# Four array quadrants per batch of 64x64 products in a chunked RWKV-7 step, and one projection step moved between the transposes

## The reference, cut

```python
SEQ = 512; HEAD_SIZE = 64; N_HEADS = 16; DEC_BATCH = 8; D_FF = 2816
def rwkv7_recurrence(state0, r, w, k, v, kk, a):
    def step(S, inp):
        r_t, w_t, k_t, v_t, kk_t, a_t = inp
        sa = jnp.einsum('bhvk,bhk->bhv', S, kk_t)
        S = (S * w_t[:, :, None, :]
             - sa[..., None] * (kk_t * a_t)[:, :, None, :]
             + v_t[..., None] * k_t[:, :, None, :])
        y = jnp.einsum('bhvk,bhk->bhv', S, r_t)
        return S, y
def token_mixer(h, shift_prev, wkv_prev, pool_prev, pos0, l, p):
    proj = jnp.einsum('btd,de->bte', h, w_in)          # r | k | v | loras | pool | gates
    y, S_new = rwkv7_recurrence(wkv_prev, r_h, hs(decay), k_h, v_h, kk_h, hs(a))
    y = ((y - mu) * lax.rsqrt(var + GN_EPS)).reshape(B, T, D_RWKV) * p['gn_w'][l] + p['gn_b'][l]
    ...
```

## Time and profile before

| | us |
|---|---|
| median of 3 runs (1501.89 to 1502.12) | 1501.95 |
| the profiled execution | 1501.0 |
| its span, first to last instruction | 1499.2 |
| PE busy | 1257.2 |
| DVE busy | 718.3 |
| ACT busy | 483.7 |

### The profile page before, as it was taken

The page is one execution under the profiler, slowest core; times in us unless marked ns, Lnnn a source line. Parts: engine busy times, 40 slices in busy tenths (PEclk is TensorE's granted clock), DMA queues, the critical chain, the costliest instruction groups (busy, mean ns, idle before and its releaser), DMA issues. The chain is left out here.

```text
span 1499.2 us, 34641 instructions
## 1 busy us (share of the span) xinstructions
PE 1257.2 (84%) x15148; PEld 1140.8 (76%) x15148; DVE 718.3 (48%) x1101; ACT 483.7 (32%) x771; POOL 87.1 (6%) x145
## 2 busy tenths in 40 slices
PE   4777999999999998678599999526999999699953
PEld 1377888888888887565599999516999999699952
DVE  2334455555555544377233232284666666722226
ACT  0343333432434323322322222104544444322211
POOL 0002021120210202010000000000000000000000
PEclk9889999999999999785699999857999999899985
DMA  8131011010110100359623232312222222133221
GB/s 276 64 85 47 4 47 49 2 49 10 41 49 2 35 2 4 116 126 291 203 86 90 84 91 74 125 56 57 85 84 84 84 84 84 38 105 89 77 85 64
DMA packets 185345, 117.26 MB, mean 78 GB/s; under 512 B 6624, under 2 KB 177430, under 8 KB 184935
## 3 DMA queue, kind: packets, MB, share of 16 engines
q1 hardware_dynamic: 185233, 115.58, 26.3%
HBM read 108.40 MB, written 7.34 MB: 77 GB/s over the span
## 5 line engine op out<-in xcount | busy, mean ns | idle before, releaser
L199 PE MATMUL PJ<-Hh,Wh 128*128 128x260 f32 (+1 forms) x1088 | 244.9, 307 | 54.1 <-DVE Wl L1725 20.3
L199 PEld LDWEIGHTS PJ<-Hh,Wh 128*128 128x128 f32 x1088 | 173.7, 194 | 73.6 <-issue 32.2
L199 PE MATMUL PJ<-Hl,Wh 128*128 128x260 f32 (+1 forms) x1088 | 224.6, 289 | 0.0
L199 PE MATMUL PJ<-Hh,Wl 128*128 128x260 f32 (+1 forms) x1088 | 223.5, 287 | 0.0
L199 PEld LDWEIGHTS PJ<-Hl,Wh 128*128 128x128 f32 x1088 | 173.4, 194 | 0.0
L199 PEld LDWEIGHTS PJ<-Hh,Wl 128*128 128x128 f32 x1088 | 173.2, 193 | 0.0
L1725 DVE TENSOR_TENSOR Wl<-RAW,Wh 128x1024 fp32r<-128x1024 f32 (+1 forms) x68 | 80.8, 1194 | 100.8 <-ACT Wh L1665 96.2
L1665 ACT ACTIVATE Wh<-RAW 128x1024 fp32r<-128x1024 f32 (+1 forms) x68 | 70.1, 1036 | 111.0 <-PE PJ L199 103.4
L1745 DVE SCALAR_TENSOR_TENSOR ACC<-ACC,CP 128x512 f32<-128x512 f32 x88 | 66.0, 750 | 69.6 <-ACT ACC L1676 68.0
L1419 DVE TENSOR_TENSOR Wl<-RAW,Wh 128x1024 fp32r<-128x1024 f32 (+1 forms) x40 | 44.7, 1119 | 112.0 <-ACT Wh L1381 111.2
L199 PE MATMUL PJ<-SFh,Wh 128*128 128x260 f32 x352 | 71.9, 286 | 13.0 <-DVE Wl L1725 13.0
(11 more groups left out here) (312 smaller groups left out, 2446.2 us busy)
## 6 DMA issues: line engine op xcount, KB each, us to landing
RAW<-in_w_in_dram SPq DMA_DIRECT2D x46, 512.0 KB, 4.1
RAW<-in_ffn_up_dram SPq DMA_DIRECT2D x44, 512.0 KB, 3.8
RAW<-in_ada_w_dram SPq DMA_DIRECT2D x32, 512.0 KB, 6.0
RAW<-in_ffn_down_dram SPq DMA_DIRECT2D x16, 512.0 KB, 4.1
RAW<-in_ada_w_dram SPq DMA_DIRECT2D x2, 2048.0 KB, 11.3
ACC<-in_ada_w_dram SPq DMA_DIRECT2D x2, 2048.0 KB, 13.5
RAW<-in_w_branch_rwkv_dram SPq DMA_DIRECT2D x8, 512.0 KB, 4.1
RAW<-in_w_out_dram SPq DMA_DIRECT2D x8, 512.0 KB, 4.1
```

What stands on the lines that cost most here:

```text
L199: mm = pe.matmul(out[:, b, 0:nb[b]], w[:, slot, kw, :], x[:, kx, c0:c0 + nb[b]], start=first and w is Wh and x is xh, stop=last and w is Wl)
```

## The change

All batches of a slot except Gram and level 0's first are rewritten so that consecutive products fall on all four quadrants. Which half of the partitions a chunk's operand lies on now alternates with `j` (`bp`, `kq`, `b_at`), and so does its PSUM bank (`x_pos`, `t_pos`), so that the two quadrants with the same target partitions write different banks. The four transpose batches become a batch of 32 products (both parts of `BK`), a projection step `dense(1)`, and a batch of 24 (`VX` and the odd chunks of `ARI`); the other 8 (`ARI` even) go behind L640 of level 1. The starting `TT` of level 1, which DVE formed from `MO` in SBUF, now comes from a further PE batch of 16 and a DVE add from PSUM. Level 5 has `dense(1)` in place of `dense(2)`, step `j` = 3 of the recurrence has only `gate`, and a `dense(1)` stands between the two last batches ahead of the recurrence: 24 steps in all, as before. ACT empties `ARI` in two parts; the second, and the copy of `mm_nv`, also wait for DVE's `tt`. ACT and DVE read and write pairs of half banks in single instructions of the same size as before. Two waits of PE on its own `mm_v` are placed differently.

```diff
+            def kq(h, j):
+                return HH[1 - (h ^ j & 1)]
+            def bp(h, j):
+                return HH[h ^ j & 1]
+            def b_at(lv, h, j):
+                return HH[h ^ (lv & 1 & (j ^ j >> 1))]
+            def x_pos(lv, j):
+                return (j >> 1 & 1, (j >> 2) * 2 + (j & 1)) if lv % 2 else (j & 1, j >> 1)
+            def t_pos(lv, j):
+                return x_pos(1, j) if lv == 1 else ((j ^ j >> 1) & 1, j >> 1)
...
-                    for b, turn in enumerate((1, 1, 0, 0)):
-                        pe.wait_ge(S("gram_ev"), 4 * c + b + 1)
-                        for j in range(NJ):
+                    pe.wait_ge(S("gram_ev"), 4 * c + 2)
+                    for j in range(NJ):
+                        at = C * (j // 2)
+                        for h in range(2):
+                            pe.matmul(B[j % 2][bp(h, j), at:at + C], BK[HH[h], j, 0, :], I2[HH[h], :], start=True, stop=True)
+                        for h in range(2):
+                            mm = pe.matmul(B[1 - j % 2][kq(h, j), 256 + at:256 + at + C], BK[HH[h], j, 1, :], I2[HH[h], :], start=True, stop=True)
+                    mm.then_inc(S("t_in"), 1)
+                    dense(1)
...
+                    pe.wait_ge(S("tr_ev"), 5 * c + 4)
+                    for j in (0, 2, 1, 3, 4, 6, 5, 7):
+                        r, q = x_pos(1, j)
+                        for h in range(2):
+                            mm = pe.matmul(B[2 + r][b_at(1, h, j), q * C:(q + 1) * C], I2[bp(h, j), :], MO[bp(h, j), 0, j, :], start=True, stop=True)
+                    mm.then_inc(S("mm_tt"), 1)
...
-                                mm = pe.matmul(B[0][HH[h], j * C:(j + 1) * C], MO[HH[h], lv % 2, j, :],
-                                               I2[HH[h], :] if lv == 0 else TI[HH[h], j, :], start=True, stop=True)
+                                mm = pe.matmul(B[r][b_at(lv, h, j), q * C:(q + 1) * C], MO[bp(h, j), lv % 2, j, :], TI[bp(h, j), ti, :],
+                                               start=True, stop=True)
...
-                        dense(2 if lv == LEVELS - 1 else 1)
+                        dense(1)
...
-                            mm = pe.matmul(B[j // 4][HH[h], (j % 4) * P:(j % 4 + 1) * P], TT[HH[h], j, :],
-                                           AW[HH[h], j, :, :].rearrange("p s t -> p (s t)"), start=True, stop=True)
+                            mm = pe.matmul(B[j % 2][bp(h, j), at:at + P], TT[HH[h], flat(t_pos(2, j)), :],
+                                           AW[HH[h], j ^ 1, :, :].rearrange("p s t -> p (s t)"), start=True, stop=True)
...
+                    dense(1)
+                    pe.wait_ge(S("mm_v"), 3 * c + 2)
...
-                        dense(1)
                         if j == 3 and nxt:
                             gate(c + 1)
+                        else:
+                            dense(1)
...
+                        if lv == 1:
+                            act.wait_ge(S("t_in"), 3 * c + 3)
+                            act.wait_ge(S("tt"), LEVELS * c + 2)
+                            act.activation(AW[:, 1::2, 0, :], B[2][:, 256:512].rearrange("p (q t) -> p q t", t=C), ACT.Copy).then_inc(S("tr_ev"), 1)
...
-                    dve.wait_ge(S("mo0"), c + 1)
-                    dve.tensor_tensor(TT[:], MO[:, 0], rows8(I2), ALU.add).then_inc(S("tt"), 1)
                     dve.wait_ge(S("mm_x"), LEVELS * c + 1)
                     dve.tensor_tensor(TI[:], bank8(0), rows8(I2), ALU.add).then_inc(S("xi"), 1)
+                    dve.wait_ge(S("mm_tt"), LEVELS * c + 1)
+                    dve.tensor_tensor(by_type(TT), pairs(0, 2), eyes, ALU.add).then_inc(S("tt"), 1)
```

More of the change, by code:

```diff
@@ new lines, in slot @@
+                    pe.wait_ge(S("xs"), num(c, V_) + 1)
+                    pe.wait_ge(S("gram_ev"), 4 * c + 4)
+                    for j in range(NJ):
+                        at = C * (j // 2)
+                        for h in range(2):
+                            mm = pe.matmul(B[3 - j % 2][kq(h, j), at:at + C], VX[HH[h], j * C:(j + 1) * C], I2[HH[h], :], start=True, stop=True)
+                        if j % 2:
+                            for h in range(2):
+                                mm = pe.matmul(B[2][HH[h], 256 + at:256 + at + C], ARI[HH[h], j, 0, :], I2[HH[h], :], start=True, stop=True)
@@ new lines, in slot @@
+                    mm.then_inc(S("t_in"), 1)
+                    pe.wait_ge(S("mo0"), c + 1)
+                    pe.wait_ge(S("tr_ev"), 5 * c + 2)
+                    for j in range(NJ):
+                        for h in range(2):
+                            mm = pe.matmul(B[0][bp(h, j), j * C:(j + 1) * C], MO[bp(h, j), 0, j, :], I2[bp(h, j), :], start=True, stop=True)
+                    mm.then_inc(S("mm_x"), 1)
+                    pe.wait_ge(S("tr_ev"), 5 * c + 4)
+                    for j in (0, 2, 1, 3, 4, 6, 5, 7):
+                        r, q = x_pos(1, j)
+                        for h in range(2):
+                            mm = pe.matmul(B[2 + r][b_at(1, h, j), q * C:(q + 1) * C], I2[bp(h, j), :], MO[bp(h, j), 0, j, :], start=True, stop=True)
@@ new lines, in slot @@
+                    mm.then_inc(S("mm_tt"), 1)
+                    if nxt:
+                        za(c + 1)
+                    for lv in range(1, LEVELS):
+                        order = sorted(range(NJ), key=lambda j: x_pos(lv, j)[::-1])
+                        pe.wait_ge(S("mo"), (LEVELS - 1) * c + lv)
+                        if lv == 1:
+                            pe.wait_ge(S("xi"), LEVELS * c + 1)
+                        else:
+                            pe.wait_ge(S("ti"), (LEVELS - 2) * c + lv - 1)
+                        for j in order:
+                            r, q = x_pos(lv, j)
+                            ti = j if lv == 1 else flat(x_pos(lv - 1, j))
@@ L625, in slot @@
                         dense(2)
+                        pe.wait_ge(S("xi"), LEVELS * c + lv + 1)
+                        pe.wait_ge(S("tt"), LEVELS * c + lv)
+                        if lv < LEVELS - 1:
+                            for j in order:
+                                r, q = x_pos(lv, j)
+                                for h in range(2):
+                                    mm = pe.matmul(B[r][bp(h, j), 256 + q * C:256 + (q + 1) * C], TT[b_at(lv, h, j), flat(t_pos(lv, j)), :],
+                                                   XI[b_at(lv, h, j), flat((r, q)), :], start=True, stop=True)
+                            mm.then_inc(S("mm_ti"), 1)
@@ L626, in slot @@
+                        if lv == 1:
+                            for j in range(0, NJ, 2):
+                                at = 256 + C * (j // 2)
+                                for h in range(2):
+                                    mm = pe.matmul(B[2][HH[h], at:at + C], ARI[HH[h], j, 0, :], I2[HH[h], :], start=True, stop=True)
+                            mm.then_inc(S("t_in"), 1)
                         if lv == 2:
-                            pe.wait_ge(S("tr_ev"), 4 * c + 4)
+                            pe.wait_ge(S("tr_ev"), 5 * c + 5)
@@ L634, in slot @@
[L634 to L641, removed]
@@ L676, in slot @@
[L676 to L681, removed]
                     if nxt:
                         bo(c + 1)
-                    pe.wait_ge(S("mm_v"), 2 * c + 2)
+                    pe.wait_ge(S("mm_v"), 3 * c + 1)
@@ new lines, in slot @@
+                    mm.then_inc(S("mm_v"), 1)
+                    dense(1)
+                    pe.wait_ge(S("mm_v"), 3 * c + 2)
+                    for j in range(NJ):
+                        at = C * (j // 2)
+                        for h in range(2):
+                            mm = pe.matmul(B[2 + j % 2][HH[h], at:at + C], W[bp(h, j), j, 1, :], BP[bp(h, j), j, 1, :], start=False, stop=False)
+                    mm.then_inc(S("mm_v"), 1)
+                    pe.wait_ge(S("mm_v"), 3 * c + 3)
```

136 lines of the change are left out of this document (70 added, 66 removed).

## The result

| us | before | after |
|---|---|---|
| median, each with its first set of runs | 1501.92 (1500.52 to 1502.12, 4 runs) | 1453.63 (1449.52 to 1456.56, 4 runs) |
| the profiled execution | 1501.0 | 1455.15 |
| its span | 1499.2 | 1453.4 |
| PE busy | 1257.2 | 1194.6 |
| DVE busy | 718.3 | 709.8 |

The changed kernel takes 0.968 of the time of the kernel before (95% interval 0.965 to 0.971), 48.3 us less. 1449 was forecast, 4.6 us less than measured. A second set, of five executions, gave 1453.86 (1451.27 to 1459.49), ratio 0.970 (0.968 to 0.971). In the first set the kernel before varies by 1.6 us and the changed one by 7.0; measured again beside the experiments, the kernel before varies by 4.3 us (9 executions) and by 5.9 (11).

What follows compares the result with a forecast made beforehand. PE's own stream was taken to bound slots 0 to 6, a dependent chain the last. Terms gave -6.5 us a slot, -45.5 for seven, -7.1 for the last: 1501.95 to 1449 us, range 1434 to 1480 (about 0.8).

Steps and rivals of the forecast that it cites:

- 2, level 1 to 2: Middle slot, level 1 to 2: three batches save 1.40 us, ARI's rest costs 0.47; -0.9, with ACT just in time.
- 3, level 2 to 3: Middle slot, level 2 to 3: four shorter batches save 1.87 us, less 0.2 for overlap already there; -1.7.
- step 4: Middle slot, level 3 to 4: R's first step waits for K's bank to empty, batches queued behind; +0.5 us, wait costs 1.9.
- 5, level 4 to 5: Middle slot, level 4 to 5: three shorter batches, -1.4 us; DVE's `key` delays XI by some 0.5 under `dense(2)`.
- 6, level 5 to `mm_w`: Middle slot, level 5 to `mm_w`: two batches save 0.93 us and one projection step fewer 0.73; -1.65.
- Step 7: Middle slot, `mm_w` to `mm_qm`: the 0.88 us saved becomes a longer wait for DVE's copy of W; 0.
- 8, to the recurrence: Middle slot, `mm_qm` to the recurrence: shorter batches, the moved step and an uncovered 0.34 us wait, 6.21 to 5.4; -0.8.
- (a): PE cannot be fed that fast: at 27.5 ns a record the kernel ends slower, 1522 us; chance 0.08.
- (b): Half of the feeding loss: 17 to 21 ns a record, 2 to 5 us less gained a slot, 1467 to 1485; chance 0.11.
- rival (c): Level 3's stall is the only loss and smaller: up to 1.5 us a slot more gained, 1438 us; chance 0.07.
- rival (d): Clock grant halves in PE's added waits: a 3.4 us stretch costs 1.7, ten give +17, 1466 us; chance 0.06.
- The last slot: Slot without projection steps: levels 1 to 5 save 4.6 us, `mm_w` 0.87, stretch to the recurrence 0.95, transposes 0.7; -7.1.

Runs made afterwards that it cites:

- the filled: Changed kernel plus three products whose results nobody reads, in PE's level 3 wait between K's last and R's first step, slots 0 to 6: 1451.53 us, 0.967.
- the fastest kernel: Changed kernel with R's first step behind level 3's batches, and chunk 7's recurrence step brought forward behind `mm_w`: 1434.35 us, 0.9547 of the kernel before.
- the other moved step: Changed kernel with the projection step ahead of the recurrence put back to chunk 3, beside `gate`: 1451.88 us, 0.967 of the kernel before.

## Why the prediction was right, step by step

The undisturbed slot 3 of both traces, from one first record to the next:

| step | before | after | forecast | measured |
|---|---|---|---|---|
| 1, transposes to level 1 (from the slot's start) | 8.69 | 8.83 | +0.1 | +0.14 |
| 2, level 1 to 2 | 6.52 | 5.62 | -0.9 | -0.90 |
| 3, level 2 to 3 | 7.29 | 5.62 | -1.7 | -1.67 |
| 4, level 3 to 4 | 6.02 | 6.51 | +0.5 | +0.49 |
| 5, level 4 to 5 | 6.57 | 5.17 | -1.4 | -1.40 |
| 6, level 5 to `mm_w` | 5.47 | 3.83 | -1.65 | -1.64 |
| 7, `mm_w` to `mm_qm` | 3.34 | 3.35 | 0 | +0.01 |
| 8, to the recurrence | 6.21 | 5.37 | -0.8 | -0.84 |
| 9, recurrence | 9.95 | 9.28 | -0.74 | -0.67 |
| slot's end | 1.85 | 1.85 | 0 | 0 |
| slot | 61.91 | 55.43 | -6.5 | -6.48 |

**The rate.** 0.0146 us a record was taken from a burst; whole batches run at 0.47 / 32 = 0.0147, three in a row without slowing. Gram's 0.0275 goes with its 128 columns: the 32 records of `mm_w`, also 128 columns, now start 0.027 us apart on four quadrants, 0.055 before. Rivals (a) and (b) fall with the table: any loss of feeding would stand in steps 3, 5 and 6. (By its own numbers the lower end of (b) is about 1463 and not 1467, and step 4 begins from 6.02 and not 5.99; nothing hangs on either.)

**The stall of step 4** came where and as long as it was forecast, 1.97 of idle time against some 1.9, and 1.94 from ACT's start to R's against 1.93, released by XK; that it was all there is to lose in a middle slot, and no smaller, is shown by the table, so rival (c) falls. That it could cost more than its own length stood in the prediction only as rival (d).

**Step 7** gave the 0 that was forecast, but the idle time stands elsewhere than the prediction said. The timeline of PE behind `mm_w` in slot 3, before and then after:

```profile
358.42 0.48 PE L199 MATMUL PJ<-Hh,Wh 128*128 128x260 f32 x2
...
359.72 1.64 PE L665 MATMUL BB<-BP,W 64*64 64x128 f32 x26 [0.33 <-DVE W L972]
```

```profile
339.70 0.48 PE L199 MATMUL PJ<-Hh,Wh 128*128 128x260 f32 x2 [0.94 <-DVE XR L943]
...
341.00 1.10 PE L727 MATMUL BB<-BP,W 64*64 64x128 f32 x32 [0.33 <-DVE W L1048]
```

The wait ahead of `mm_qm` for W, which was to grow, is 0.33 in both. What took up the 0.88 is the wait ahead of V's first step, until DVE has written XR and with it emptied R's bank: 0.94 against 0.08. Both waits hang on one chain from the end of projection R, through ACT, DVE's XR and DVE's copy of W, as the prediction had it, which is why the 0 came out. It is the same kind of wait as K's in step 4.

**The last slot** is -6.73 against -7.1: levels 1 to 5 -4.34 (4.6 forecast), the stretch to level 1 -0.55 (0.7), the other two -0.84 and -1.02 (0.87 and 0.95). A level of 3.03 instead of 2.95 is 0.08 of hand-over in each, and the transposes of that slot gave less.

**What was mis-sized is the sum over the slots**: seven times 6.5 was 45.5; measured 38.1, 7.4 less. Two causes:

1. Rival (d), the clock, at part size. Four stretches instead of ten, at 1.5 us each (56.9 against 55.43) where 1.7 was taken, so 6.0 us less gained, of which before had one of 1.6, in its slot 6: net 4.4. The argument against it was slot 7, which waits in each level and keeps the full grant. It was a poor witness: its waits are some 0.8 us each, and in the filled and the fastest kernel this slot has 6.8 us of half clock after all. The better witness was in the trace of before itself, the stretch in slot 6 behind a wait of 1.5 us.
2. Slot 0. It gained 2.27 where slot 3 gained 6.48, 4.2 less; its stretch of half clock is 1.5 of that. The timeline of PE in that slot shows where the other 2.7 are:

```profile
133.85 1.14 PE L548 MATMUL PJ<-TWA,WL 64*128 64x260 f32 x4 [2.11 <-DMA WG<-in_gate_up_dram]
...
141.59 0.56 PE L672 MATMUL BB<-TI,MO 64*64 64x64 f32 x20 [0.37 <-issue]
...
151.36 0.33 PE L704 MATMUL BB<-TT,RAW 64*64 64x64 f32 x3 [1.09 <-issue]
```

   PE waits for the first load of WG as it did before (1.74), and the time gained doesn't shorten a wait for a transfer; this is 0.4 of the 2.7. The rest are two stops in the middle of a batch, in `mm_x` of level 1 and in `mm_tt` of level 2, for which PE waits for nothing that the profile shows: with them level 1 to 2 gained 0.2 instead of 0.9, and level 2 to 3 gained 0.1 instead of 1.7. The kernel before has no such stop there; most other traces with four quadrants have one or both. Their cause stays open. The forecast gave slot 0 the full 6.5. In the second set this slot is 56.77, without the second stop and without half clock, so this term varies between executions by about 3 us.

4.4 and 2.7 are 7.1 of the 7.4; 0.24 more is slot 1, and the rest is rounding.

The last slot adds 0.4, and the blocks ahead and behind give back 1.0. So the span shrank by 45.8 where 52.6 was forecast; the median by 48.3, since the profiled execution of the changed kernel, at 1455.15, lies 1.5 above its median and that of before 0.9 below. That the forecast of 1449 lies only 4.6 from the median is thus in part luck: between the two profiled executions the gain is 6.8 less than forecast.

The spread of the changed kernel, 7 us against 1.6, may seem to go with these drops, which differ between two executions (slots 0, 2, 4, 6 and then 1, 4, 6 and 7). The runs don't bear that out: the other moved step, which keeps the wait, varies by 3.2 us in five executions, and the fastest kernel, which does not have it, by 13.0 in six. What sets the spread isn't shown.

## What to carry to other kernels

Small products on TensorE's quadrants gain from all four only if neighbours in the program's order are on unlike quadrants: spread each batch over both diagonals and alternate, for the order was worth about 40 us here, 5.9 us a slot, and the spreading without it 2.8 a slot. When batches get shorter, look again at what hid behind them: a projection step in front of the batches that used to cover the emptying of its bank became a wait of 1.97 us that ate more than the gain of its level, and two steps placed by hand gave some 20 us more. A wait of 2 us on a TensorE that is otherwise full is to be priced above its own length: behind 14 of 35 such waits came a stretch of half clock that cost 1.5 us.

## What the runs showed of the hardware that was not expected

- Four quadrants with 64 columns each sustain a record every 0.0148 us over 96 records. The Trainium skill, page "TensorE: Matmul & The Clock Gate", section "Wait — 56ns, not 53.3ns?", gives about 25 ns as the least distance of two starts; by that rule the changed kernel would have come to about 1508 us, which is the prediction's estimate, and these rows disagree.
- Records of two diagonals queued one behind the other overlap only for the few around the seam, some ten within 0.17 us, and there they start out of the program's order: grouped batches run at 0.76 us, alternating ones at 0.47.
- Half clock for 3.4 us followed waits of 1.97 us (14 of 35, in five traces) and of 1.52 us (5 of 63, in nine), with PE at full clock for long before, at some slots and not at others with the same instructions. A wait of 0.88 or 0.66 in place of the 1.97 was followed by none in slots 0 to 6 (28 waits, four traces). Length alone does not decide: the wait of 1.6 to 2.2 us for the load of WG in slot 0 had none directly behind it in ten traces. What decides between two equal slots stays open.
